# Split weights in four parts of 1024 columns in place of two slabs of 2048

## The reference

```python
for i in range(DEPTH):
    h = rms_norm(x, W['norm_mix_pre'][i])
    if i < N_A:
        m, st = conformer_conv(h, conv_prev[i], ...)
    else:
        c_kv, k_rope = shared_kv(x, pos, ...)
        q_lat, q_rope = mla_query(h, pos, ...)
        o_lat = prompt_attention(q_lat, q_rope, c_kv, k_rope, pos)
        m = mla_output(o_lat, W['w_uv'], W['w_o'][j])
    x = x + rms_norm(m, W['norm_mix_post'][i])
    h = rms_norm(x, W['norm_ff_pre'][i])
    x = x + rms_norm(sq_relu_mlp(h, W['w_up'][i], W['w_down'][i]), W['norm_ff_post'][i])
    x = x + jax.nn.sigmoid(x @ W['ple_gate'][i]) * (ple[i] @ W['ple_proj'][i])
```

## Time and profile before

| | us |
|---|---|
| median of 3 runs (2096.03 to 2097.19) | 2096.18 |
| the profiled execution | 2097.72 |
| its span in the profile | 2095.9 |
| TensorE busy (88% of the span) | 1835.1 |
| GpSimd busy (43%) | 910.8 |
| VectorE busy (42%) | 886.4 |
| ScalarE busy (33%) | 701.5 |

### The profile page before, as it was taken

One profiled execution on the slowest core, in us unless ns is written; L12 is line 12 of the kernel. 1 busy time (PEld: TensorE's weight loads), 2 busy tenths in 40 slices (PEclk: granted clock), 3 DMA queues, 4 the chain that ended last, 5 costly groups with the idle time before them and its releaser, 6 DMA issues.

```text
span 2095.9 us, 34419 instructions
## 1 busy us (share of the span) xinstructions
PE 1835.1 (88%) x12386; PEld 1641.1 (78%) x12386; DVE 886.4 (42%) x1840; ACT 701.5 (33%) x1367; POOL 910.8 (43%) x594
## 2 busy tenths in 40 slices
PE   5766368899999996887989989999989999999968
PEld 4765248899999995886966646666778999999968
DVE  4698852422222227646344444444233222222284
ACT  4454543322222233443212233333233222222332
POOL 3787626655555555456310000000166555555651
PEclk9887679899999998997988979999889999999979
DMA  4510011122222220221300205555511222222201
GB/s 109 141 41 21 22 52 61 61 80 80 80 80 85 94 81 21 84 66 31 119 4 1 69 23 159 158 156 159 172 61 61 80 86 90 84 80 80 80 1 46
DMA packets 154006, 160.26 MB, mean 76 GB/s; under 512 B 32409, under 2 KB 116979, under 8 KB 153922
## 3 DMA queue, kind: packets, MB, share of 16 engines
q1 hardware_dynamic: 148896, 153.19, 23.9%
q10 hardware_dynamic: 5026, 6.02, 1.0%
HBM read 154.39 MB, written 4.79 MB: 76 GB/s over the span
## 4 chain that ended last, share of the span: by engine, by line
PE 70%; DVE 12%; POOL 7%; issue 5%; ACT 4%; DMA 1%; DVEq 1%; ACTq 0%; SPq 0%; POOLq 0%
PE bank L1641 18%; PE bank L1642 18%; PE bank L1643 18%; PE bank L2068 4%; PE bank L2102 3%; PE bank L2026 3%; DVE X L1194 2%; DVE bank L1248 2%; POOL WL L1000 2%; POOL acc L1014 1%; PE bank L1967 1%; DVE AL L1162 1%; POOL R L1066 1%; PE bank L1948 1%; DMA RAW<-in_conv_pw 1%
## 5 line engine op out<-in xcount | busy, mean ns | idle before, releaser
L1000 POOL TENSOR_TENSOR WL<-RAW,WH 128x2048 fp32r<-128x2048 f32 (+1 forms) x106 | 481.2, 4540 | 836.8 <-ACT WH L552 836.3
L1641 PE MATMUL bank<-AH,WH 128*128 128x288 f32 x2112 | 655.3, 310 | 146.1 <-DVE scaled L1227 49.7
L1642 PE MATMUL bank<-AL,WH 128*128 128x288 f32 x2112 | 642.8, 304 | 0.0
L1643 PE MATMUL bank<-AH,WL 128*128 128x288 f32 x2112 | 641.7, 304 | 0.0
L1641 PEld LDWEIGHTS bank<-AH,WH 128*128 128x128 f32 x2112 | 415.5, 197 | 167.4 <-issue 77.5
L1642 PEld LDWEIGHTS bank<-AL,WH 128*128 128x128 f32 x2112 | 417.3, 198 | 0.1
L1643 PEld LDWEIGHTS bank<-AH,WL 128*128 128x128 f32 x2112 | 416.3, 197 | 0.0
L1641 PE MATMUL bank<-BH,WH 128*128 128x288 f32 (+1 forms) x1120 | 338.2, 302 | 9.1 <-DVE BL L1334 5.1
L1642 PE MATMUL bank<-BL,WH 128*128 128x288 f32 (+1 forms) x1120 | 336.3, 300 | 0.0
L1643 PE MATMUL bank<-BH,WL 128*128 128x288 f32 (+1 forms) x1120 | 336.1, 300 | 0.0
L552 ACT ACTIVATE WH<-RAW 128x2048 fp32r<-128x2048 f32 (+1 forms) x106 | 199.0, 1877 | 373.9 <-PE bank L1643 354.8
(11 more groups left out here) (244 smaller groups left out, 2054.5 us busy)
## 6 DMA issues: line engine op xcount, KB each, us to landing
RAW<-in_w_up SPq DMA_DIRECT2D x32, 1024.0 KB, 5.5
RAW<-in_w_down SPq DMA_DIRECT2D x32, 1024.0 KB, 5.1
RAW<-in_cache_kv_latent SPq DMA_DIRECT2D x128, 256.0 KB, 2.8
RAW<-in_conv_pw SPq DMA_DIRECT2D x16, 512.0 KB, 7.4
RAW<-in_ple_gate SPq DMA_DIRECT2D x8, 1024.0 KB, 5.2
RAW<-in_conv_pw SPq DMA_DIRECT2D x4, 1024.0 KB, 5.2
RAW<-in_cache_k_rope SPq DMA_DIRECT2D x128, 32.0 KB, 2.8
RAW<-in_w_o SPq DMA_DIRECT2D x4, 1024.0 KB, 5.2
```

What stands on the lines that cost most here:

```text
L1000: nc.gpsimd.tensor_tensor(WL[:, d % WRING, 0:n], raw_of(d), WH[:, d % WRING, 0:n].bitcast(F32), ALU.subtract).then_inc(lo_done, 1)
L1641: nc.tensor.matmul(out, wh, xh, start=first, stop=False)
L1642: nc.tensor.matmul(out, wh, xl, start=False, stop=False)
L1643: return nc.tensor.matmul(out, wl, xh, start=False, stop=last)
```

## The change

WH and WL become four slots of 1024 columns. Each slab is handled as two parts, part q holding one half of the slab's output tiles for all inner rows (in the key/value slabs: the key half and the value half; the small dkv slab is one part). `hi` and `lo` run once a part, each with its own count of `hi_done` and `lo_done`; a part's slot waits for the units that read the part four before; TensorE waits for `lo_done` before each unit, for the part that the unit reads. A part is read from RAW as eight (four, six, two) runs of a tile's columns and stored packed. The last MLP chunk leaves the loops of ScalarE and GpSimd and is written out behind them, since the slab after it has another shape. Places that counted slabs now count parts, which the cut diff leaves out where nothing else changes.

```diff
@@ -51,9 +51,9 @@
-RING, WRING = 4, 2
+RING, WRING = 4, 4
 SLOT = 4 * (CL + DR)
-WSLOT = 2048
+WSLOT, WPART = 2048, 1024
...
+def slab_shape(kind, j):
+
+    if kind[:3] == "mlp":
+        return (KT, 256) if j % 4 < 2 else (FC, 512)
+    if kind[:3] == "ple":
+        return 2, D
+    if kind == "uq":
+        return QL // P, 256
+    return (KT, P) if (kind, j) == ("dkv", 2) else (KT, 256)
+
+
+DENSE = [(g, k, j) for g, (k, j) in enumerate(KIND) if k not in ("cache", "uv")]
+PART0, PART_AT = [], []
+for _d, (_g, _k, _j) in enumerate(DENSE):
+    PART0.append(len(PART_AT))
+    PART_AT += [(_d, _q) for _q in range(1 if (_k, _j) == ("dkv", 2) else 2)]
+PART0.append(len(PART_AT))
...
-        WH, WL = sb("WH", [P, WRING, WSLOT], F32R), sb("WL", [P, WRING, WSLOT], F32R)
+        WH, WL = sb("WH", [P, WRING, WPART], F32R), sb("WL", [P, WRING, WPART], F32R)
...
@@ -355,7 +374,7 @@
-                sp.wait_ge(lo_done, DENSE0[kind] + j + 1)
+                sp.wait_ge(lo_done, PART0[DENSE0[kind] + j + 1])
...
+        def part_width(d):
+
+            kt, n = slab_shape(*DENSE[d][1:])
+            return kt, n // (PART0[d + 1] - PART0[d])
+
+        def raw_part(d, q):
+
+            g, kind, j = DENSE[d]
+            if kind == "kvh":
+                return RAW[:, g % RING, q * WPART:(q + 1) * WPART]
+            kt, w = part_width(d)
+            n = slab_shape(kind, j)[1]
+            return RAW[:, g % RING, 0:kt * n].rearrange("p (k n) -> p k n", k=kt)[:, :, q * w:(q + 1) * w]
+
+        def split_part(t, d, q):
+
+            r = (PART0[d] + q) % WRING
+            if DENSE[d][1] == "kvh":
+                return t[:, r, :]
+            kt, w = part_width(d)
+            return t[:, r, 0:kt * w].rearrange("p (k n) -> p k n", k=kt)
...
-        def used_at(d):
-
-            _, kind, j = dense_slabs[d]
+        def used_at(d, q):
+
+            _, kind, j = DENSE[d]
             if kind == "kvh":
-                return kvt_done, 2 * j + 2
+                return (v_mm, j + 1) if q else (kvt_done, 2 * j + 2)
+            u = UNIT0[kind]
             if kind in ("mlp0", "mlp1"):
-                return unit_done, UNIT0[kind] + CHUNK * (j // 4) + (4, 8, 16, 24)[j % 4]
-            if kind == "dkv":
-                return unit_done, UNIT0[kind] + (4, 8, 10)[j]
-            return unit_done, UNIT0[kind] + UNITS[kind] // SLABS[kind] * (j + 1)
+                return unit_done, u + CHUNK * (j // 4) + (3 + q, 7 + q, 14 + 2 * q, 22 + 2 * q)[j % 4]
+            if kind[:3] == "ple":
+                return unit_done, u + 12 + 4 * q
+            if (kind, j) == ("dkv", 2):
+                return unit_done, u + 10
+            return unit_done, u + 4 * j + 3 + q
 
         @block.scalar
         def _(act):
-            def hi(d, i=None, per=16):
+            def hi(d, i=None):
 
                 s, v = landed_at(d)
-                act.wait_ge(s, v if i is None else v + per * i)
-                if d >= WRING:
-                    s, v = used_at(d - WRING)
-                    act.wait_ge(s, v if i is None else v + (16 if KIND[dense_slabs[d][0]][0] == "pw1" or d == 8
-                                                            else CHUNK) * i)
-                elif i is not None:
-                    act.wait_ge(bank_free, BANKS + 16 * i)
-                nc.scalar.activation(WH[:, d % WRING, 0:slab_size(d)], raw_of(d), ACT.Copy).then_inc(hi_done, 1)
+                act.wait_ge(s, v if i is None else v + 16 * i)
+                for w in range(PART0[d], PART0[d + 1]):
+                    q = w - PART0[d]
+                    if w >= WRING:
+                        s, v = used_at(*PART_AT[w - WRING])
+                        if i is not None:
+                            v = max(v, used_at(*PART_AT[w - WRING + 2 * RING])[1] - CHUNK)
+                        act.wait_ge(s, v if i is None else v + CHUNK * i)
+                    nc.scalar.activation(split_part(WH, d, q), raw_part(d, q), ACT.Copy).then_inc(hi_done, 1)
...
@@ -743,9 +778,9 @@
                 phase, v = f"mlp{layer}", f"g{layer}"
                 d0, u0, stx = DENSE0[phase], UNIT0[phase], f"x{2 * layer + 1}"
                 b0 = UP * NCH * layer
-                with act.Fori(0, NCH) as i:
+                def chunk(i):
                     for j in range(4):
-                        hi(d0 + j + 1, i)
+                        hi(*((d0 + j + 1, i) if type(i) is not int else (d0 + 4 * i + j + 1,)))
                         if j == 3:
                             for h in range(2):
                                 act.wait_ge(acc_done, SQ(stx, h, 0) - 2 + 2 * i)
@@ -766,6 +801,9 @@
                                 act.wait_ge(bank_free, freed(u0 + n) + CHUNK * i)
                                 nc.scalar.activation(half(BH, 2 * j + q % 2, q // 2), prod[:, n % 2, :], ACT.Copy)\
                                     .then_inc(u_hi, 1)
+                with act.Fori(0, NCH - 1) as i:
+                    chunk(i)
+                chunk(NCH - 1)
...
@@ -995,10 +1033,11 @@
         @block.gpsimd
         def _(pool):
             def lo(d, i=None):
-                pool.wait_ge(hi_done, d + 1 + (0 if i is None else RING * i))
-                n = slab_size(d)
-                nc.gpsimd.tensor_tensor(WL[:, d % WRING, 0:n], raw_of(d), WH[:, d % WRING, 0:n].bitcast(F32),
-                                        ALU.subtract).then_inc(lo_done, 1)
+                for w in range(PART0[d], PART0[d + 1]):
+                    q = w - PART0[d]
+                    pool.wait_ge(hi_done, w + 1 + (0 if i is None else 2 * RING * i))
+                    nc.gpsimd.tensor_tensor(split_part(WL, d, q), raw_part(d, q), split_part(WH, d, q).bitcast(F32),
+                                            ALU.subtract).then_inc(lo_done, 1)
 
             def add(st, h, m):
 
...
@@ -1642,17 +1684,20 @@
                 nc.tensor.matmul(out, wh, xl, start=False, stop=False)
                 return nc.tensor.matmul(out, wl, xh, start=False, stop=last)
 
-            def wslab(d, kt, n, k, c):
-
-                a = k * n + c
-                return WH[:, d % WRING, a:a + P], WL[:, d % WRING, a:a + P]
+            def wpart(d, k, t):
+
+                w = part_width(d)[1]
+                q, c = divmod(t * P, w)
+                r, a = (PART0[d] + q) % WRING, k * w + c
+                return WH[:, r, a:a + P], WL[:, r, a:a + P]
 
             def rows(src, k, h):
 
                 return half(src[0], k, h), half(src[1], k, h)
 
-            def slab_ready(d, i=None):
-                pe.wait_ge(lo_done, d + 1 if i is None else d + 1 + RING * i)
+            def ready(d, t, i=None):
+                w = PART0[d] + t * P // part_width(d)[1] + 1
+                pe.wait_ge(lo_done, w if i is None else w + 2 * RING * i)
...
-            def product(phase, kt, n, tiles, v, src=None, after=(), between=None):
+            def product(phase, kt, v, src=None, after=(), between=None):
 
                 u = UNIT0[phase]
                 for j in range(SLABS[phase]):
                     d = DENSE0[phase] + j
-                    slab_ready(d)
-                    w = n[j] if isinstance(n, tuple) else n
-                    nt = w // P
+                    nt = slab_shape(phase, j)[1] // P
                     for h in range(2):
                         for t in range(nt):
-                            def ready(k, h=h):
+                            b = bank[u % BANKS][:, 0:H]
+                            ready(d, t)
+                            pe.wait_ge(bank_free, u + 1)
+                            for k in range(kt):
                                 if v and j == 0 and t == 0:
                                     pe.wait_ge(a_lo, A(v, h, k))
-                            b = bank[u % BANKS][:, 0:H]
-                            pe.wait_ge(bank_free, u + 1)
-                            for k in range(kt):
-                                ready(k)
-                                ins = three(b, wslab(d, kt, w, k, t * P), rows(src or Asrc, k, h), k == 0,
-                                            k == kt - 1)
+                                ins = three(b, wpart(d, k, t), rows(src or Asrc, k, h), k == 0, k == kt - 1)
...
@@ -1806,9 +1847,9 @@
                 with pe.Fori(0, NCH) as i:
                     n = 0
                     for j in range(4):
-                        slab_ready(d0 + j, i)
                         for h in range(2):
                             for t in range(2 if j < 2 else 4):
+                                ready(d0 + j, t, i)
                                 pe.wait_ge(bank_free, u0 + n + 1 + CHUNK * i)
                                 dst = bank[(u0 + n) % BANKS][:, 0:H]
                                 for k in range(KT if j < 2 else FC):
@@ -1817,10 +1858,10 @@
                                     if j == 2 and t == 0:
                                         pe.wait_ge(u_lo, b0 + up_n(h, k) + 3 + UP * i)
                                     if j < 2:
```

(29 more changed lines are left out.)

34 lines of the change are left out of this document (14 added, 20 removed).

## The result

Four runs of the changed kernel took 2056.21 to 2069.53 us, median 2062.27, against 2096.68 before: a ratio of 0.9835 (95% interval 0.9802 to 0.9869), 34.4 us faster. These four runs of the kernel before lie 3 us apart (later sets of it 5 to 11), those of the changed one 13, and that spread turned out to be part of the answer. The profile is of the slowest of the four (2069.53), 28.2 us under the profiled execution of before. One run of all that follow, of `moved_fill`, took 2454.22 us at a granted clock of 0.696 and stands in no median.

A forecast was written before the change was run, and what follows sets the result against it. TensorE was taken to bound the MLPs, busy throughout, leaving gains only at the seams: stage starts, attention and first convolution. Shortened waits summed to 24.6 us, taken from the median 2096.18 to give 2071.6 us, range 2064 to 2085.

The forecast's parts named there:

- Sum: 8.8 + 2.0 + ... = 24.6: Whole kernel: gains at attention, query, embedding, MLP starts and latents, convolution and gates, less 0.2 us of cost, total 24.6 us.
- The three waits: Attention, heads 0, 2 and 4: TensorE's 3.48 us waits for VectorE's normalising shrink by 2.95 each, 8.8 us in all.
- VectorE slips in: Attention: VectorE, asking 0.14 us before the first half of `lo` ends, runs between the two halves; 2.95 us each.
- first rival: VectorE is not let in between the halves, or asks too late: attention gives 1.7, query 1.0; 2079.7 us, chance 0.25.
- Query stage, 2.0: Query up-projection: the rotation's last sum on VectorE finishes before TensorE is idle, removing its 2.00 us wait.
- Embedding, 2.7 each: Before the embedding stage, both layers: the projection slab's split ends earlier, cutting TensorE's 3.96 us wait; 5.4 us in all.
- MLP starts and latents, 5.3: MLP starts and latent projection: TensorE needs only the first part; three waits gain 2.1 + 1.3 + 1.9 us.
- First convolution tile, 2.1: First layer's convolution: an earlier `lo` stops delaying GpSimd additions, so VectorE's 2.15 us idle goes; 2.1 us.
- Gates, 0.6 each: Gate starts, both layers: VectorE's first product, just too late, waits for the second half, which ends earlier; 1.2 us.
- The edit's own costs: Smaller parts, reads in runs and 448 new TensorE waits: nothing in the MLPs; 0.17 us per pair in places, -0.2 counted.
- slower rival: TensorE pays one matmul slot for each of 448 new waits: 59.6 us lost, 24.6 gained; 2131 us, chance 0.05.
- likeliest case: The forecast itself, chance 0.47, with its bounds on the embedding stage: 2069 to 2077 us.

The follow-up runs named there:

- moved_fill: `moved` with four matmuls whose result nobody reads in each of three attention waits of 1.08 us; 2051.63 us (ratio 0.9783).
- before_fill: The kernel before, with fourteen matmuls whose result nobody reads in each of its three waits of 3.48 us; 2084.13 us (ratio 0.9937).
- late_fill: `late` with nine matmuls whose result nobody reads in each of its three attention waits; 2065.30 us (ratio 0.9846).
- between: The changed kernel, with the copy of the key/value slab's second part moved behind the fourth exponent and the next probability copy in heads 0, 2, 4; 2060.63 us.
- halves: The kernel before, with only `lo` as two instructions of half the columns and one signal behind the second; 2085.90 us (ratio 0.9938).
- late: The changed kernel, with ScalarE's copy of the next head's keys made in two halves so that VectorE asks later; 2076.29 us (ratio 0.9893).
- again: The changed kernel unedited, timed again on a first further occasion; median 2072.52 us (ratio 0.9881).
- again2: The changed kernel unedited, timed on a second further occasion; median 2065.96 us (ratio 0.9860).
- again3: The changed kernel unedited, timed on a third further occasion; median 2069.56 us (ratio 0.9859).
- moved: `between` with a gate-slab copy moved behind two sigmoids and the second query slab's `lo` held until VectorE has turned the keys; 2054.17 us (ratio 0.9789).

## Why the forecast was wrong, point by point

- **The step that failed** is the sum itself: "Sum: 8.8 + 2.0 + ... = 24.6", a sum of waits at their own length. It puts the clock behind the waits at nothing, without a reason; the only clock that it read is that of the MLP, 1.00. At the seams it is not: behind each 3.48 of the earlier trace rows the trace had 6.8 to 10.2 us at half clock. The three waits were to give 8.8, and the clock behind them is worth some 10 by itself (`before_fill`, `late_fill`). With no misses the attention alone gives 8.9 + 11.1 = 20 us (`between`), of which 4.1 at its end are not explained.
- **"VectorE slips in", with a margin of 0.14.** The margin measured 0.10, and that is where it is decided anew each time: four in twelve. The mechanism of the earlier trace rows is right where VectorE asks well ahead (1.03 in `halves`), and the first rival's where it asks 0.04 ahead (`late`). So forecast and rival were both true, in different heads of one run. The rule that I set against the earlier trace rows (the Trainium skill, SBUF — State Buffer, Who interferes with whom: issue order decides) does not shut VectorE out wherever a second half follows, as I had read it. By the recorded starts VectorE is 0.99 us ahead of the second half in `halves` and is let in, and just behind it in `late` and is not: both agree. At 0.05 to 0.06 ahead, four in twelve, these starts do not tell which was issued first.
- **Query stage, 2.0:** it gave 0.3. The half starts 0.64 earlier, as worked out, but so it meets the operation ahead of L1452 first (L1450, 2.08 instead of its usual 0.75), and L1452 then asks into the second half (2.26). I had moved GpSimd's instruction and looked only at the one VectorE instruction that it had blocked before.
- **Embedding, 2.7 each:** 3.97 and 3.96 became 1.21, 2.75 each: right. In layer 0 part of it is given back in the residual update behind it, where the matmuls run at half clock (+2.5 of spacing); in layer 1 spacing fell instead, and no run here isolates why.
- **MLP starts and latents, 5.3:** 5.6 became 0.2: right. **First convolution tile, 2.1:** VectorE's idle of 2.15 is gone, and the convolution's waits are 2.4 less: right (2.4 to 4.4 in the four profiles of this kernel, so other waits move there too). **Gates, 0.6 each:** 2.49 and 2.48 became 1.79 and 1.80: right.
- **The edit's own costs:** parts take 2.418 and 1.051, the 448 new waits show nowhere in the MLP: nothing, as taken. The slower rival falls.

By the same count over all stretches the waits of the unedited kernel gave 19.5 us (first profile), 22.4 (`again`), 21.7 (`again2`) and 19.8 (`again3`), and its spacing 9.2, 5.4, 18.0 and 2.4. That the median of the 18 runs, 2069.3, is near the forecast's 2071.6 is thus luck, two errors against each other; and that the first four lie lower, at 2062.27, is the draw of these four, since the other 14 have 2069.6. The forecast's 2069 as lower end of its likeliest case follows from none of its bounds (the embedding's upper one is 2.76 for 2.7). Open: what decides between two askings alike to 5 ns, and why the end of the attention was longer at half clock in the trace before.

## What to carry to other kernels

Price a wait of TensorE with the stretch behind it: look up the granted clock there, and add what runs at 0.50 at half its length at most; here 27.2 us cost 10.1. Where two engines exclude each other, a margin of a tenth of a microsecond is no margin: move the instruction until it is clear, as in `between` and `moved`, whose runs lie 5.6 and 3.1 us apart where those of the changed kernel lie 6 to 16. When an instruction on one engine moves, go through all operations of the other that it now overlaps, not only the one it had blocked.

## What the runs showed of the hardware that I had not expected

Waits of TensorE of 2.6 to 2.7 us in heads 0, 2 and 4 were each (14 in six traces) followed by 6.8 to 10.2 us at half clock. So were shorter ones: 1.32 us in `halves` (3.4 to 6.8, three in three) and 1.08 in head 4 of `between` and `moved` (6.8, one in three each), but none of the four of 0.48 to 0.49. Matmuls for nothing in the wait kept the clock full and made the kernel before 13.6 us faster. And VectorE asking 0.09 to 0.11 us ahead of the end of one GpSimd instruction, with another right behind it, was let in four times in twelve, for no reason that the records show.
